# A wide moving operand, a transposed inverse taken from its mate, and a reciprocal moved ahead

## What is computed

```python
# first block, time mix
kk = (k * k_k).reshape(B, S, H, N)
kk = kk / jnp.maximum(jnp.linalg.norm(kk, axis=-1, keepdims=True), 1e-12)
k = k * (1.0 + (a - 1.0) * k_a)                    # the modified keys
# per token: state = state*w + (state @ -kk)[...,None]*(kk*a) + v[...,None]*k ;  y = state @ r
# first block, feed-forward (D_FF = 2816)
f = (jax.nn.silu(h @ w_ffn_gate) * (h @ w_ffn_up)) @ w_ffn_down
# second block, feed-forward (4096 wide)
f = jnp.square(relu(h @ w_up)) @ w_down
```

## Time and profile before

| | |
|---|---|
| median of three runs | 852.21 us |
| the profiled execution | 853.91 us |
| its span, first to last instruction | 852.0 us |
| TensorE busy | 839.8 us, 7276 matmul records |
| DVE busy | 546.1 us |
| ACT busy | 394.4 us |
| mean granted TensorE clock | 0.995 |
| HBM traffic | 138.69 MB read |

### The profile page before, as it was taken

The page is one execution under the profiler, slowest core; times in us unless marked ns, Lnnn a source line. Parts: engine busy times, 40 slices in busy tenths (PEclk is TensorE's granted clock), DMA queues, the critical chain, the costliest instruction groups (busy, mean ns, idle before and its releaser), DMA issues.

```text
span 852.0 us, 16571 instructions
## 1 busy us (share of the span) xinstructions
PE 839.8 (99%) x7276; PEld 773.3 (91%) x7276; DVE 546.1 (64%) x606; ACT 394.4 (46%) x457; POOL 5.9 (1%) x8
## 2 busy tenths in 40 slices
PE   9999999999999999999999999999999999999997
PEld 8989889898989999999999989988998999999996
DVE  5998755546788655555557656595754765566554
ACT  6652331366367434343447354446544533344432
POOL 0000010000000000000000000000000000000000
PEclk9998999999999999999999999999999999999999
DMA  9845513131674665646553754536433465555531
GB/s 299 282 150 177 167 54 102 54 99 53 241 244 132 198 199 196 194 151 200 194 198 100 246 170 136 175 124 206 176 103 123 140 228 174 180 193 183 178 133 49
DMA packets 97002, 140.62 MB, mean 165 GB/s; under 512 B 2480, under 2 KB 79408, under 8 KB 96944
## 3 DMA queue, kind: packets, MB, share of 16 engines
q1 hardware_dynamic: 96512, 139.36, 50.0%
q10 hardware_dynamic: 432, 0.39, 0.2%
HBM read 138.69 MB, written 1.05 MB: 164 GB/s over the span
## 4 chain that ended last, share of the span: by engine, by line
PE 88%; DVE 6%; ACT 2%; issue 2%; DMA 2%; SPq 0%; ACTq 0%; DVEq 0%
PE PS L427 86%; DMA raw<-in_w_in_dram 2%; DVE wlo L1627 2%; PE PS L530 1%; ACT whi L1201 1%; DVE rw L1689 1%; DVE diff L1686 0%; DVE stg L1684 0%; DVE Gm L1781 0%; ACT st L1201 0%; PE PS L673 0%; PE PS L1037 0%; DVE cs L1706 0%; DVE wlo L1664 0%; DVE krs L1719 0%
## 5 line engine op out<-in xcount | busy, mean ns | idle before, releaser
L1627 DVE TENSOR_TENSOR wlo<-raw,whi 128x2048 fp32r<-128x2048 f32 x122 | 279.4, 2291 | 136.8 <-ACT whi L1201 136.5
L1201 ACT ACTIVATE whi<-raw 128x2048 fp32r<-128x2048 f32 (+1 forms) x130 | 241.2, 1858 | 181.3 <-PE PS L427 177.7
L427 PE MATMUL PS<-xh,whi 128*128 128x256 f32 x1136 | 322.4, 287 | 0.9 <-ACT xh L1201 0.7
L427 PE MATMUL PS<-xh,wlo 128*128 128x256 f32 x1136 | 317.2, 284 | 0.1
L427 PE MATMUL PS<-xl,whi 128*128 128x256 f32 x1136 | 315.2, 284 | 0.0
L427 PEld LDWEIGHTS PS<-xh,whi 128*128 128x128 f32 x1136 | 217.9, 193 | 5.9 <-issue 3.3
L427 PEld LDWEIGHTS PS<-xh,wlo 128*128 128x128 f32 x1136 | 217.2, 193 | 0.3 <-DVE wlo L1664 0.3
L427 PEld LDWEIGHTS PS<-xl,whi 128*128 128x128 f32 x1136 | 215.7, 193 | 1.1
L427 PE MATMUL PS<-whi,fh 128*128 128x512 f32 x216 | 84.4, 391 | 0.0
L427 PE MATMUL PS<-wlo,fh 128*128 128x512 f32 x216 | 84.4, 391 | 0.0
L427 PE MATMUL PS<-whi,fl 128*128 128x512 f32 x216 | 84.1, 389 | 0.0
(11 more groups left out here) (310 smaller groups left out, 1045.0 us busy)
## 6 DMA issues: line engine op xcount, KB each, us to landing
raw<-in_w_in_dram SPq DMA_DIRECT2D x32, 1024.0 KB, 5.3
raw<-in_w_up_dram SPq DMA_DIRECT2D x16, 1024.0 KB, 5.3
raw<-in_w_down_dram SPq DMA_DIRECT2D x16, 1024.0 KB, 4.9
raw<-in_w_ffn_gate_dram SPq DMA_DIRECT2D x11, 1024.0 KB, 5.3
raw<-in_w_ffn_up_dram SPq DMA_DIRECT2D x11, 1024.0 KB, 5.4
raw<-in_w_ffn_down_dram SPq DMA_DIRECT2D x11, 1024.0 KB, 5.0
raw<-in_w_kv_mem_dram SPq DMA_DIRECT2D x8, 1024.0 KB, 5.4
raw<-in_w_o_dram SPq DMA_DIRECT2D x4, 1024.0 KB, 8.0
```

Of the source, the lines that this page charges most:

```text
L427: return nc.tensor.matmul(o, l, r, start=start, stop=stop, **kw)
L1201: return nc.scalar.activation(o, i, f, **kw)
L1627: V.tensor_tensor(wlo[u % RING][:], raw[u % RING][:], whi[u % RING][:].bitcast(f32), ALU.subtract) \
```

## The change

xh and xl become two views of one tile, so that for one slice of the depth the 256 high and 256 low tokens lie side by side. `by_feature_wide` uses both as one moving operand of 512 columns against whi, and 256 columns of xh against wlo. The two parts of a result land in two halves of a bank. ACT copies the second halves, DVE adds the first, and then scales. It is used for all chunks but the first in both feed-forwards. Banks are used anew: gate 0 and 1, up 2 and 3.

In the inverse (`turned` of one level is issued inside `lower` of the next, between the halves of a gate unit; the fifth in `amid(6)`) TT is no longer joined by products of its own: `turned(v)` multiplies Tm by the identity, and DVE copies the new columns into TT. `lower` makes only the 32 columns that the mask keeps. `join` makes only Tm's part, at the fifth level too. The AK products go ahead of the first level (banks 6 and 7), the value transposes behind levels 2 and 3 (bank 7, one tile of tokens each), AK by values ahead of the sixth gate unit, WT behind it, (it waits for `tt_ready` 6), AV by TT ahead of the seventh (it waits for WT's evacuation), and k_tok's evacuation on ACT behind the exponential and `hi`.

At i == 5 DVE inverts the key norms first and makes the modified keys afterwards.

```diff
+        xhl = at("xhl", A0, [P, KD, 2, SEQ], f32r)
+        xh, xl = xhl[:, :, 0], xhl[:, :, 1]
...
+            def by_feature_wide(u, both, b, later=0):
+                n = units[u][1]
+                wh, wl = split(u, n, later)
+                for f in range(2):
+                    fs = slice(f * P, (f + 1) * P)
+                    for k in range(KD):
+                        mm(bank(b + f), wh[:, k, fs], both[:, k].rearrange("p a t -> p (a t)"), k == 0, False, skip_group_check=True)
+                    for k in range(KD):
+                        last = mm(bank(b + f)[:, 0:SEQ], wl[:, k, fs], both[:, k, 0], False, k == KD - 1, skip_group_check=True)
+                last.then_inc(sem("units_used"), 1)
...
             def lower(v):
...
+                if v == 1:
+                    pe.wait_ge(sem("tt_ready"), 1)
+                else:
+                    turned(v - 1)
+                if v == 6:
+                    return
+                for ... in out_of(XT[half(c), c ^ tt, s_, :], halves(Tm[half(c), c ^ tt, s_, :], v, 0)):
+                    last = mm(PS[h, b * 512 + s_ * n:b * 512 + (s_ + 1) * n], l, r, True, True)
...
+            def turned(v):
+                for ... in out_of(Tm[half(c), c ^ tt, s_, :], halves(C("ident")[half(c), half(c)], v, 1)):
+                    last = mm(PS[h, b * 512 + 256 + s_ * n:b * 512 + 256 + (s_ + 1) * n], l, r, True, True)
+                last.then_inc(sem("turn_mm"), 1)
...
             def join(v):
                 pe.wait_ge(sem("g_ready"), v)
+                pe.wait_ge(sem("tt_ready"), v)
...
             def before(i):   # TensorE
                 if i == 1:
                     tokens(eX, 0, "tok_T", True)
+                    pairs(eN, eX, "pair_mm", 6)
...
+                        if i == 1:
+                            pe.wait_ge(sem("ff_gate"), 1)
+                        else:
+                            pe.wait_ge(sem("gate_sum"), i - 1 + FF_BODY * n)
+                        by_feature_wide(U_F["g", i], xhl, 0, later)
...
+                            pe.wait_ge(sem("up_sum"), i - 1 + FF_BODY * n)
+                        by_feature_wide(U_F["u", i], xhl, 2, later)
...
+                        by_feature_wide(U_M["u", i], xhl, 2 - 2 * (i % 2), later)
...
             def ffn(i, n=0):   # ACT
                 hi(U_F["g", i] + RING, n, FF_STEP)
+                if i:
+                    act.wait_ge(sem("units_used"), U_F["g", i] + 1 + FF_STEP * n)
+                    second_halves(fa[i % 2], 0).then_inc(sem("gate_second"), 1)
                 act.wait_ge(sem("ff_gate"), i + 1 + later)
                 A_(fa[i % 2][:], fa[i % 2][:], ACT.Silu).then_inc(sem("ff_silu"), 1)
+                if i:
+                    act.wait_ge(sem("units_used"), U_F["u", i] + 1 + FF_STEP * n)
+                    second_halves(fb[i % 2], 2).then_inc(sem("up_second"), 1)
...
                 if i == 5:
+                    dve.wait_ge(sem("kk_sd"), 1)
+                    link(V.tensor_scalar(krs[:], krs[:], 1e-12, None, ALU.max))
+                    V.reciprocal(krs[:], krs[:]).then_inc(sem("kk_rs"), 1)
+                if i == 5:
...
             def lower_out(v):   # DVE
+                if v > 1:
+                    dve.wait_ge(sem("turn_mm"), v - 1)
+                    for x in range(2):
+                        last = V.tensor_copy(halves(TT[:, x]..., v - 1, 1), bank(2 + x)[:, 256:512]...)
+                    last.then_inc(sem("tt_ready"), 1)
...
             def ffn(i, n=0):   # DVE
+                if i:
+                    dve.wait_ge(sem("gate_second"), i + later)
+                    summed(fa[i % 2], 0).then_inc(sem("gate_sum"), 1)
+                    dve.wait_ge(sem("gate_sum"), i + later)
+                V.tensor_tensor(pair(fa[i % 2]), pair(fa[i % 2]) if i else two(0), spread(rs), ALU.mult).then_inc(sem("ff_gate"), 1)
                 lo(U_F["g", i] + RING, n, FF_STEP)
```

More of the change, by code:

```diff
@@ L721, in join @@
[L721 to L728, removed]
+                for c, tt, s_, h, b, l, r in back_to(lambda c, tt, s_: TT[half(c ^ tt), c, s_, :],
+                                                     lambda c, tt, s_: halves(Gm[half(c ^ tt), c, s_, :], v, 0)):
+                    last = mm(PS[h, b * 512 + s_ * n:b * 512 + (s_ + 1) * n], l, r, True, True)
@@ new lines, in amid @@
+            def amid(i):
+                if i == 0:
+                    pe.wait_ge(sem("sv_ready"), 2)
+                    pe.wait_ge(sem("rw_pre"), 1)
+                    pairs(kk, eX, "pair_mm")
+                    pairs(kk, eX, "pair_mm", 6, True)
+                elif i < 6:
+                    if i == 1:
+                        pe.wait_ge(sem("tok_ready"), 1)
+                    lower(i)
+                elif i == 6:
+                    pe.wait_ge(sem("chunk_ready"), 1)
+                    lower(6)
+                else:
+                    pe.wait_ge(sem("chunk_ready"), 3)
+                    tokens(eN, 0, "tok_T")
+                    pe.wait_ge(sem("sb_arg_read"), NPAIR)
+                    pairs(eN, eP, "pair_mm", 4)
@@ new lines, in behind @@
+            def behind(i):
+                if i == 0:
+                    pe.wait_ge(sem("pair_ready"), 1)
+                    pairs(eX, kk, "pair_mm")
+                elif i < 6:
+                    join(i)
+                    if i in (2, 3):
+                        pe.wait_ge(sem("pair_ready"), 4)
+                        pe.wait_ge(sem("tok_ready"), i - 1)
+                        for j in range(NPAIR):
+                            last = nc.tensor.transpose(PS[:, 7 * 512 + j * P:7 * 512 + (j + 1) * P],
+                                                       rw[:, 8 + j, (i - 2) * P:(i - 1) * P], C("ident"))
+                        last.then_inc(sem("tok_T"), 1)
+                elif i == 6:
@@ L757, in before @@
                     last.then_inc(sem("chunk_mm"), 1)
[L758 to L762, removed]
-                if i == 0:
-                    pe.wait_ge(sem("sv_ready"), 2)
-                    pe.wait_ge(sem("rw_pre"), 1)
-                    pairs(kk, eX, "pair_mm")
-                    pairs(kk, eX, "pair_mm", 6, True)
[L769 to L782, removed]
-                else:
-                    pe.wait_ge(sem("sb_arg_read"), NPAIR)
-                    pairs(eN, eP, "pair_mm", 4)
-            def behind(i):
-                if i == 0:
-                    pe.wait_ge(sem("pair_ready"), 1)
-                    pairs(eX, kk, "pair_mm")
[L792 to L800, removed]
+                else:
+                    pe.wait_ge(sem("tok_ready"), 4)
                     tokens(kk, 0, "tok_T")
@@ L1336, in bank_pair, with values_tile @@
                 last.then_inc(sem(done), 1)
+            def values_tile(tt):
+                act.wait_ge(sem("tok_T"), 2 + tt)
+                A_(vt_[:, tt, :], bank(7), ACT.Copy).then_inc(sem("tok_ready"), 1)
             def gate_sigmoid(c):
@@ L1998, in _, with summed @@
             dve.wait_ge(norm_sem("n2", "rs"), nth("n2", "rs", 1))
+            def summed(dst, b):
+                o = PS[:, b * 512:(b + 2) * 512].rearrange("p (f a t) -> p f a t", f=2, a=2)
+                return V.tensor_tensor(pair(dst), o[:, :, 0], pair(dst), ALU.add)
             def ffn(i, n=0):
@@ L2009, in ffn @@
                     dve.wait_ge(sem("ff_hi"), i - 1 + later)
-                V.tensor_tensor(pair(fb[i % 2]), two(2 * (i % 2) + 1), spread(rs), ALU.mult).then_inc(sem("ff_up"), 1)
+                if i:
+                    dve.wait_ge(sem("up_second"), i + later)
+                    summed(fb[i % 2], 2).then_inc(sem("up_sum"), 1)
+                    dve.wait_ge(sem("up_sum"), i + later)
+                V.tensor_tensor(pair(fb[i % 2]), pair(fb[i % 2]) if i else two(2), spread(rs), ALU.mult).then_inc(sem("ff_up"), 1)
                 dve.wait_ge(sem("ff_up"), i + 1 + later)
@@ L2172, in mlp @@
                     dve.wait_ge(sem("mlp_sq"), i - 1 + later)
-                V.scalar_tensor_tensor(out=pair(fa[i % 2]), in0=two(i % 2 if i else 2), scalar=0.0, in1=spread(rs), op0=ALU.max, op1=ALU.mult) \
+                if i:
+                    dve.wait_ge(sem("mlp_second"), i + later)
+                    summed(fa[i % 2], 2 - 2 * (i % 2)).then_inc(sem("mlp_sum"), 1)
+                    dve.wait_ge(sem("mlp_sum"), i + later)
+                V.scalar_tensor_tensor(out=pair(fa[i % 2]), in0=pair(fa[i % 2]) if i else two(2), scalar=0.0, in1=spread(rs), op0=ALU.max, op1=ALU.mult) \
                     .then_inc(sem("mlp_out"), 1)
```

124 lines of the change are left out of this document (69 added, 55 removed).

## The result

The changed kernel takes 839.89 us (median of four runs, 839.43 to 840.58) against 852.23 for the kernel before beside it: ratio 0.9856, 95% interval 0.9839 to 0.9873. The forecast was 834.6 with a range of 832.9 to 839.6, so the gain was 12.3 us where 17.6 were expected. The profiled execution took 840.33 us with a span of 838.5, 13.5 less than before.

What follows compares the result with a forecast made beforehand. The prediction took TensorE's own instruction stream, not its waits, to bound the kernel. Savings of 7.6 + 5.9 + 4.2 = 17.7 us took the span from 852.0 to 834.3 us; forecast median 834.6, range 832.9 to 839.6.

Steps and rivals of the forecast that it cites:

- Part 3: Reciprocal first at i == 5: TensorE's 1.18 us wait before krs and the slow clock behind it go, 4.2 us gained.
- rival (a): Around the krs spread: slow clock stays or returns, brought by the 8-row products, not the gap; 837.7 us, chance 0.09.
- Part 2: Turned inverse in the chunk stage: 4.8 us less TensorE work and 1.1 us less waiting, 5.9 us gained.
- 15 groups at the price of the 32-column group: Inverse, five levels of lower, turned and join: each group at 0.96 us, 14.4 us against 19.2, saving 4.8.
- waits on Gm: Inverse: TensorE's three waits for DVE's Gm, 1.3 us together, shrink to about 0.1 at even levels, none at odd.
- WT wait of 0.3: Before the WT products: a new TensorE wait of 0.3 us, since WT needs the last turned half.
- (b): Inverse bound by DVE and ACT: Gm late by about 0.5 us at five levels, WT and AV 0.5 each; 838.1 us, chance 0.09.
- Part 1: Wide operand in both feed-forwards: 32 matmuls per converted unit become 16 of 512 columns, 7.6 us gained over 35 units.
- term of 0.217 us: Saving per converted feed-forward unit, from 16 pairs going from 0.240 to 0.2264 us each; 35 units give 7.6 us.
- (c): Feed-forwards: the wide matmul gains nothing, a pair keeps its 0.240 us; 842.2 us, chance 0.05.
- (d): Feed-forward loops: the chain of the halves binds at the next up unit's low part; 869.5 us if 4.5 later, chance 0.03.
- (e): Inverse: the edit fails to do what it says, turned falls to two quarters of the array; 839.7 us, chance 0.02.

Runs made afterwards that it cites:

- before_allrows: The kernel before, with the eight krs spread records reading 128 rows (zero from row 8 on) and the gap kept: 850.71 us, ratio 0.9980.
- after_allrows: The changed kernel, with the eight krs spread records reading 128 rows (zero from row 8 on) instead of 8: 839.30 us.

## Why the prediction was wrong

The direction, the three mechanisms on TensorE's path and the absence of any new wait in the loops were right (the third only for the gap, not for the clock). Each term of 7.6 + 5.9 + 4.2 was too large; against the median they gave 6.6, 3.8 and 1.8.

- **Part 3, the step that failed: "With it, I think, goes the slow clock, which nothing but this gap precedes".** The 8-row records stand right behind the gap, and they were dismissed as rival (a), with a chance of 0.09, because the narrow products at 40 us keep the clock. But those are narrow in columns (they give 8) and read all 128 rows; these read 8 rows and give 128 columns. With 128 rows the slow stretch is gone, with the gap (before_allrows) and without it (after_allrows). Rival (a) was the truth here: its 837.7 was then raised by the shortfalls of parts 1 and 2.
- **The same step, its size.** 3.1 us of slow clock came from an execution whose slow stretch was the longer of the usual ones, and the whole was taken from the median, 1.7 us lower, in which by its mean clock it was shorter. Even a complete cure would have been worth 1.7 us by the medians (before_allrows). A term that differs between executions can't be read off one profile and taken from a median.
- **Part 2, "15 groups at the price of the 32-column group, 14.4 us".** The earlier trace rows show that price once, and there a like group follows. Ahead of anything else it is 1.04 to 1.07. Eleven of the 15 stand there, so the sum was 15.45: 1.05 us lost. The waits on Gm went as worked out or better (0.05 us left over at two joins), and the WT wait of 0.3 hid behind the pause.
- **Part 2, what was missed.** 1.44 us of instruction fetch. No step of the prediction looked at q8. With it the part is accounted for: 5.9 - 1.05 - 1.44 + 0.4 (the waits that didn't come) = 3.8, as measured. The rival that came nearest in time, (b), named the wrong engine: neither DVE nor ACT was late.
- **Part 1, the term of 0.217 us.** The wide step itself was right, 227 ns from a row in which the operands are swapped, and (c) falls. The change from narrow to wide was taken as free; it costs 28 ns, against 7 that come back on the other change. The trace has 46 of the first and 70 of the second, 0.8 us, and the old unit got 8 ns back 23 times behind by_token, 0.2 us: 1.0 together, which is also what the medians lack (6.6 of 7.6).
- **The loops (d) and the two quarters (e)** were rightly low.

The range ended 0.3 us short of the result. Its own bounds for parts 2 and 3 (3.2 and 1.1 us) give 834.6 + 2.7 + 3.1 = 840.4 together. They had been weighed one at a time, each with a small chance, and in truth three terms fell low at once.

## What to carry to other kernels

When a slow clock follows two things, a gap and a thin product, test both: padding a small contraction with zero rows costs TensorE nothing (from the first of the eight records to the next unit it is 1.85 us in `after_allrows` and 1.92 in the changed kernel) and tells which it was. When a stretch of many tiny matmuls is moved or shortened, look at where its blocks of instructions fall against the bulk loads; a load can be shifted or cut where it isn't wanted yet. And take the price of a group from a row with the same neighbours, and a gain from the same kind of execution as the base it is taken from.

## What the runs showed of the hardware

- Four float32 products over 8 rows with 256 moving columns (eight records, 1.9 us) bring TensorE's clock from 2.4 to 1.2 GHz for 3.4 or 6.8 us: in all seven profiled executions that have them, and, to judge by the times, not in every one. With 128 rows it fell in none of seven profiled executions, and the times scatter by 0.8 us at most, against 5.3 for the kernel before over all its runs (3.7 beside `before_allrows`). The engine counts as busy in both. Eight records over 8 rows with 128 moving columns (1.1 us) left the clock alone in all 14 traces.
- A packet of instructions mostly waits for the weights ahead of it: 97 of 109 began in the last 0.8 us of the load, and at the ten pauses TensorE went on 2.3 to 2.6 us after the late one began.
- Steps of 512 columns are 227 ns among their like and up to 236 for five steps behind steps of 256 columns.
